# Sums of squares later in TensorE's order, and block 0's keys turned by VectorE and exchanged through DRAM

## The reference

```python
mod = silu(c) @ w_ada + b_ada                    # shift, scale, gate
h = rms_norm(x, norm_g) * (1 + scale) + shift
proj = h @ w_in                                  # u, z_pool, q, k, v, o, z_m, gates: 7 x 512 + 8 columns
pool_out = causal_pool_mixer(u, w_pool, ls_pool) * silu(z_pool)
qk = silu(causal_depthwise_conv(q | k))          # width 4
hm = mlstm_chunkwise(q, k, v, ig, lf)            # 4 heads x 128, chunks of 128 positions
mlstm_out = head_norm(hm) * sigmoid(o) * silu(z_m)
x = x + gate * (concat(pool_out, mlstm_out) @ w_out)
return rms_norm(x, final_g)
```

## Time and profile before

| what | us |
|---|---|
| three runs: median (lowest to highest) | 1813.13 (1810.76 to 1817.83) |
| the profiled execution, whole | 1815.33 |
| its span in the trace | 1813.5 |
| PE busy | 1766.9 (97%) |
| DVE busy | 1070.1 (59%) |
| ACT busy | 600.4 (33%) |
| POOL busy | 272.8 (15%) |
| mean granted clock of TensorE | 0.992 of full |

### The profile page before, as it was taken

One profiled execution on the slowest core, in us unless ns is written; L12 is line 12 of the kernel. 1 busy time (PEld: TensorE's weight loads), 2 busy tenths in 40 slices (PEclk: granted clock), 3 DMA queues, 4 the chain that ended last, 5 costly groups with the idle time before them and its releaser, 6 DMA issues.

```text
span 1813.5 us, 25007 instructions
## 1 busy us (share of the span) xinstructions
PE 1766.9 (97%) x9129; PEld 1515.1 (84%) x9129; DVE 1070.1 (59%) x2213; ACT 600.4 (33%) x1430; POOL 272.8 (15%) x229
## 2 busy tenths in 40 slices
PE   6999999999999999999999999999999999999998
PEld 5877878888898888988888887888889888898886
DVE  6685685536836288353873458553684627835383
ACT  3345352343523234222432224232342323422221
POOL 3443122040310013000130002200021000300000
PEclk9899999999999999999999999999999999999999
DMA  9796875798557774686748766478664777456652
GB/s 329 269 331 176 233 193 175 185 259 304 140 187 211 209 237 111 215 229 189 214 120 251 229 192 164 163 215 233 205 151 177 215 195 241 125 202 206 189 172 82
DMA packets 392158, 368.32 MB, mean 203 GB/s; under 512 B 256780, under 2 KB 298724, under 8 KB 392036
## 3 DMA queue, kind: packets, MB, share of 16 engines
q1 hardware_dynamic: 376836, 344.05, 62.9%
q10 hardware_dynamic: 15200, 22.68, 4.4%
HBM read 304.59 MB, written 62.06 MB: 202 GB/s over the span
## 4 chain that ended last, share of the span: by engine, by line
PE 68%; DVE 17%; DMA 6%; ACT 3%; issue 3%; SPq 2%; ACTq 0%; POOL 0%; DVEq 0%; POOLq 0%
PE ps_acc L590 19%; PE ps_acc L592 19%; PE ps_acc L591 19%; DMA sb_kT<-hm_kept 2%; DMA sb_x_in<-x 2%; PE ps_kv L590 2%; PE ps_kv L591 2%; PE ps_kv L592 2%; DVE sb_shifted L1714 1%; DMA hm_kept<-sb_kT 1%; DVE sb_silu_zp L1678 1%; PE ps_num L590 1%; DVE sb_kT L1672 1%; PE ps_num L592 1%; DVE sb_acc_cv L1714 1%
## 5 line engine op out<-in xcount | busy, mean ns | idle before, releaser
L590 PE MATMUL ps_acc<-sb_hT_hi,sb_w_split 128*128 128x512 f32 x1536 | 606.2, 395 | 1.4 <-POOL sb_w_split L1196 1.4
L592 PE MATMUL ps_acc<-sb_hT_hi,sb_w_split 128*128 128x512 f32 x1536 | 599.2, 390 | 0.0
L591 PE MATMUL ps_acc<-sb_hT_lo,sb_w_split 128*128 128x512 f32 x1536 | 598.6, 390 | 0.0
L592 PEld LDWEIGHTS ps_acc<-sb_hT_hi,sb_w_split 128*128 128x128 f32 x1536 | 288.6, 188 | 61.0
L590 PEld LDWEIGHTS ps_acc<-sb_hT_hi,sb_w_split 128*128 128x128 f32 x1536 | 288.9, 188 | 60.3 <-POOL sb_w_split L1196 1.5
L591 PEld LDWEIGHTS ps_acc<-sb_hT_lo,sb_w_split 128*128 128x128 f32 x1536 | 289.1, 188 | 57.4
L1207 POOL TENSOR_TENSOR sb_h_rs<-sb_h_var,sb_mhalf 128x4 f32<-128x4 f32 x32 | 40.9, 1279 | 1037.4 <-DVE sb_h_var L1661 1037.4
L1196 POOL TENSOR_TENSOR sb_w_split<-sb_w_raw,sb_w_split 128x512 fp32r<-128x512 f32 (+1 forms) x64 | 88.3, 1387 | 193.8 <-ACT sb_w_split L869 193.7
L1561 DVE SCALAR_TENSOR_TENSOR sb_acc_cv<-sb_shifted,sb_par,sb_acc_cv 128x512 f32<-128x512 f32 x96 | 76.9, 801 | 60.7 <-ACT sb_acc_cv L1038 58.2
L1591 DVE TENSOR_TENSOR sb_oz<-sb_tanh,sb_oz 128x512 f32<-128x512 f32 x32 | 22.2, 693 | 145.2 <-ACT sb_tanh L1054 145.2
L590 PE MATMUL ps_acc<-sb_wo_hi,sb_mixm_hi 128*128 128x512 f32 x256 | 102.9, 402 | 0.0
(11 more groups left out here) (233 smaller groups left out, 2968.8 us busy)
## 6 DMA issues: line engine op xcount, KB each, us to landing
sb_w_split<-w_kept SPq DMA_DIRECT2D x328, 512.0 KB, 4.6
sb_w_split<-w_kept SPq DMA_DIRECT2D x56, 520.0 KB, 4.3
w_kept<-sb_w_split SPq DMA_DIRECT2D x40, 512.0 KB, 5.2
sb_x_res<-x SPq DMA_DIRECT2D x34, 512.0 KB, 5.1
sb_w_raw<-w_in SPq DMA_DIRECT2D x64, 256.0 KB, 4.8
out<-sb_qT SPq DMA_DIRECT2D x32, 512.0 KB, 2.9
sb_x_in<-x SPq DMA_DIRECT2D x112, 128.0 KB, 3.9
sb_ada_raw<-w_ada SPq DMA_DIRECT2D x8, 1024.0 KB, 9.6
```

The costliest lines, as they stand in the source:

```text
L590: pe.matmul(dst, st_hi, mv_hi, start=start, stop=False)
L591: pe.matmul(dst, st_hi, mv_lo, start=False, stop=False)
L592: return pe.matmul(dst, st_lo, mv_hi, start=False, stop=stop)
```

## The change

The sums of squares: `x_sums(0)` of the next block moves from after `numerator_and_update(2)` to between tile u 3 and tile zp 3. `x_sums(1)` stays after `numerator_and_update(3)` but writes to the bank `sco`. `x_sums(2)` and `(3)` move from after `out_p(1)` and `out_p(3)` to between `out_m(2)` and `out_p(2)`, and between `out_m(4)` and `out_p(4)`. With them move, on VectorE, `prep_var(0)` (from ahead of the `k_w` product of chunk 3 to behind `windows(3)`) and `prep_var(2)` and `(3)` (behind `out_var` and `m_low`); `prep_turn(0)` now stands ahead of `y_low(3)`. On ScalarE `prep_scale(2)` and `(3)` move one output tile later, on GpSimd `x_rsqrt(2)` and `(3)` behind the output's `rsqrt`.

The keys of block 0: `keys_transposed` is gone; block 0 does what the other blocks do. VectorE turns the keys at t = 8 to 11, SP writes them (16 DMAs) at m = 33 to 39 and reads them back at m = 41, 45, 49, 53. `load_keys(0, 0)`, which writes `k_w`, waits until all of them are kept and until `fold_mm` has come to 8. The wait for `wout_scaled` moves into `numerator_and_update(0)`, ahead of L806.

```diff
-        x_sums_at = [bro[:, 0:NC]] * 3 + [kv[1][:, 384:384 + NC]]
+        x_sums_at = [bro[:, 0:NC], sco[:, 0:NC], bro[:, 0:NC]] + [kv[1][:, 384:384 + NC]]
...
             def keep_keys(b, h):
-                sp.wait_ge(keys_turned, (b - 1) * NH + (h + 1))
+                sp.wait_ge(keys_turned, b * NH + (h + 1))
...
                 if j == 0:
-                    sp.wait_ge(keys_kept_done, 256 * b)
+                    sp.wait_ge(keys_kept_done, 256 * (b + 1))
+                    if b == 0:
+                        sp.wait_ge(fold_mm, 2 * NH)
...
-                    if m in (33, 35, 37, 39) and not first:
+                    if m in (33, 35, 37, 39):
                         keep_keys(b, (m - 33) // 2)
-                    if m in (41, 45, 49, 53) and not first:
+                    if m in (41, 45, 49, 53):
                         load_keys(b, (m - 41) // 4)
...
                     tile("u", j)
-                    if first:
-                        keys_transposed(j)
+                    if j == 3 and not last_block:
+                        x_sums(b + 1, 0)
                     tile("zp", j)
                     numerator_and_update(j)
-                    if j >= 2 and not last_block:
-                        x_sums(b + 1, j - 2)
+                    if j == 3 and not last_block:
+                        x_sums(b + 1, 1)
...
                     if i > 1:
                         out_m(i)
+                    if i in (2, 4) and not last_block:
+                        x_sums(b + 1, i // 2 + 1)
                     out_p(i)
-                    if i in (1, 3) and not last_block:
-                        x_sums(b + 1, i // 2 + 2)
...
                     if i in (0, 2, 4) and not last_block:
                         prep_hi(b + 1, i)
                         prep_hi(b + 1, i + 1)
+                    if i in (2, 4) and not last_block:
+                        prep_scale(b + 1, i // 2 + 1)
...
-                    if i in (1, 3) and not last_block:
-                        prep_scale(b + 1, i // 2 + 2)
...
-                    if i in (1, 3) and not last_block:
-                        x_rsqrt(b + 1, i // 2 + 2)
                     if i % 2:
                         j = i // 2
                         rsqrt(o_var_done, b * NC + (j + 1), o_rs[:, j % 2:j % 2 + 1], o_var[:, j % 2:j % 2 + 1], o_rs_done)
+                    if i in (1, 3) and not last_block:
+                        x_rsqrt(b + 1, i // 2 + 2)
...
-                    if 8 <= t < 12 and not first:
+                    if 8 <= t < 12:
                         in_turn()
                         V.transpose(keys_squared[t - 8].rearrange("p (c n) -> p c n", n=P), kT[:, :, t - 8, :]).then_inc(keys_turned, 1)
...
-                    if first:
-                        dve.wait_ge(k_T, j + 1)
-                        keys = kv[1][:, :].rearrange("p (h d) -> p h d", d=P)
-                    else:
-                        dve.wait_ge(keys_loaded[j % 2], 16 * ((b - 1) * 2 + (j // 2 + 1)))
...
-                y_low(3)
                 if not last_block:
                     prep_turn(b + 1, 0)
+                y_low(3)
```

More of the change, by code:

```diff
@@ L268, in build @@
         tanh_ready, qk_ready, o_tanh = sem("tanh_ready"), sem("qk_ready"), sem("o_tanh")
-        pooled_ready, k_T, d_exp, k_w_ready = sem("pooled_ready"), sem("k_T"), sem("d_exp"), sem("k_w_ready")
+        pooled_ready, d_exp, k_w_ready = sem("pooled_ready"), sem("d_exp"), sem("k_w_ready")
         num_done, kv_done, h_ready, c_done = sem("num_done"), sem("kv_done"), sem("h_ready"), sem("c_done")
@@ L783, in heads_to_scores @@
                     last.then_inc(sco_full, 1)
-                def keys_transposed(j):
-                    if j == 0:
-                        pe.wait_ge(wout_scaled, KT)
-                    reach(pe, c_done, j)
-                    for h in range(NH):
-                        last = pe.transpose(kv[1][:, chunk(h)], kT[:, j, h, :], ident)
-                    last.then_inc(k_T, 1)
                 def numerator_and_update(j):
@@ L804, in numerator_and_update @@
                     pe.wait_ge(k_w_ready, b * NC + (j + 1))
+                    if first and j == 0:
+                        pe.wait_ge(wout_scaled, KT)
                     for h in range(NH):
@@ L1118, in one_block @@
                         act.wait_ge(shifted_free, b * 8 + 8)
-                        reach(act, keys_kept_done, 256 * b)
+                        act.wait_ge(keys_kept_done, 256 * (b + 1))
                     act.activation(shifted[:, 0, HALO:], src[:, :], ACT.Copy).then_inc(free, 1)
@@ L1592, in one_block @@
                         did(free, b * (TASKS // 2) + (TASK[name, i] // 2 + 1))
-                    if 8 <= t < 12 and not first:
+                    if 8 <= t < 12:
                         in_turn()
                         V.transpose(keys_squared[t - 8].rearrange("p (c n) -> p c n", n=P), kT[:, :, t - 8, :]).then_inc(keys_turned, 1)
-                        did(keys_turned, (b - 1) * NH + (t - 7))
+                        did(keys_turned, b * NH + (t - 7))
                     if t == 0:
@@ L1755, in one_block @@
                         head_norm(j - 1)
-                    if j == 3 and not last_block:
-                        prep_var(b + 1, 0)
                     in_turn()
-                    if first:
-                        dve.wait_ge(k_T, j + 1)
-                        keys = kv[1][:, :].rearrange("p (h d) -> p h d", d=P)
-                    else:
-                        dve.wait_ge(keys_loaded[j % 2], 16 * ((b - 1) * 2 + (j // 2 + 1)))
-                        keys = kT[:, j - 1, :, :] if j else k_w[:, :, :]
-                    V.tensor_tensor(k_w[:, :, :], keys, rows(expo[:, 1, NH * j:NH * j + NH]), ALU.mult).then_inc(k_w_ready, 1)
+                    dve.wait_ge(keys_loaded[j % 2], 16 * (b * 2 + (j // 2 + 1)))
+                    V.tensor_tensor(k_w[:, :, :], kT[:, j - 1, :, :] if j else k_w[:, :, :], rows(expo[:, 1, NH * j:NH * j + NH]), ALU.mult).then_inc(k_w_ready, 1)
                     did(k_w_ready, b * NC + (j + 1))
@@ L1771, in one_block @@
                     if j == 0:
-                        reach(dve, keys_kept_done, 256 * b)
+                        dve.wait_ge(keys_kept_done, 256 * (b + 1))
                     windows(j)
+                    if j == 3 and not last_block:
+                        prep_var(b + 1, 0)
                     if j == 2:
@@ L1832, in one_block @@
                         out_norm(i // 2 - 1)
-                    if i in (1, 3) and not last_block:
-                        prep_var(b + 1, i // 2 + 2)
                     if i % 2:
@@ L1841, in one_block @@
                         m_low(2 + i // 2)
+                    if i in (1, 3) and not last_block:
+                        prep_var(b + 1, i // 2 + 2)
                     if i == 2:
```

## The result

The changed kernel takes 1821.76 us (median of 10 runs, 1819.71 to 1824.66), the kernel before 1812.51 us (median of 10, 1809.81 to 1817.83). The ratio is 1.0042, 95% interval 1.003 to 1.0053: slower by some 7.6 us by this ratio, 9.25 us by the two medians. That is inside the wide range of 1805 to 1824, but 5.8 us above the 1816 that was forecast and just outside the forecast's own range, 1811 to 1821. The profiled execution of the changed kernel took 1820.55 us, with a span of 1818.7 us against 1813.5.

A forecast was written before the change was run, and what follows sets the result against it. TensorE, busy 97% of the span, was taken as the bound. From the profiled 1815.33 us, + 5.2 (block 0) - 0.9 (steady waits) - 3.1 (clock) gave 1816.5; forecast 1816, own range 1811 to 1821, wide range 1805 to 1824.

The forecast's parts named there:

- The bound and what takes its place: Blocks 1 to 6, out tile 2: x_sums waits go, add_residual(0) ends next; gain capped at 4.25 us, 0.9 us kept.
- The shift on VectorE: Block ends: prep_turn(0) ahead of y_low(3) makes everything behind it 0.65 us later, or 1.15 with the longer x_rsqrt.
- TensorE's own time: Later places of x_sums have room: x_sums(2) comes 2.7 us behind its old place, the longest wait was 2.55.
- The clock: Block 4: the fall to 1.2 GHz for 6.2 us after a 2.55 us wait goes; 3.1 us gained.
- The pair of gaps that was forecast for block 4: Block 4: one gap becomes two, 1.1 us at out_p(0) and about 1.4 at out tile 2.
- The bound that 2.20 us pass without a fall: After block 0's 2.20 us wait the granted clock stayed 1.00, so block 4's shorter new gaps should not lower it.
- Block 0: SyncE's queue: load_keys(0, 0) holds raw units 42 and 43, delaying out tile 2 to 272.05; 5.2 us lost (4.5 to 9.0).
- Unit 42's own delay: Block 0: its load lands 5.5 us after issue, so its split comes at 198.0, 6.5 us late (5.8 to 10.3).
- The keys' other costs: Block 0: four VectorE transposes and 16 stores by SyncE, taken as 0 us, bounds 0 to 2.8.
- (A): Rival, plain gain: block 0's delay hidden and nothing comes in place of the waits; 1799.2 us, chance 0.13.
- (B): Rival, slower by the clock: new gaps drop TensorE to 1.2 GHz in block 0 and two steady blocks; 1825.8 us, chance 0.13.
- (C): Rival: squares of part 2 still end last at the new place and the waits stay; 1820.5 us, chance 0.06.

The follow-up runs named there:

- the sums alone: Against the kernel before: only the sums of squares and what moves with them on VectorE, ScalarE and GpSimd moved; block 0's keys stay with TensorE; ratio 0.9995.
- the run with part 0 early: Changed kernel with x_sums(0), x_sums(1) and prep_var(0) in their old places, prep_turn(0) still ahead of y_low(3); ratio 1.0001 to the kernel before.
- the load behind x: Changed kernel with block 0's first load of keys issued behind raw units 42, 43 and the next x's eight loads; ratio 0.9998 to the kernel before.

## Why the prediction came out as it did

**The bound and what takes its place.** Right. TensorE's waits at `x_sums` went and waits for `add_residual(0)` came: 5.0 us in six places. Steady blocks were to give 0.9 + 3.1 = 4.0 us; the profiled pair gives 3.6. But that agreement is partly luck. Block by block the differences are +1.18, +0.43, +0.30, -5.38, +0.49 and -0.63, where 0.2 to 0.5 of gain and one block at -3.1 were forecast. The step treated one execution's waits, 0.70, 0.66, 2.55 and so on, as if the next execution had them again; they hang on the wait for the heads, which differs from block to block and between executions. The half with the sums alone, 0.9995 (0.9985 to 1.0004) or 1 us, is the better measure of this step. It fits the 0.9; the 4.0 with the clock's 3.1 lies outside it (0.9985 is 2.7 us).

**The shift on VectorE.** Right to the hundredth. In block 2 the instructions ahead of the old place of `prep_var(0)` stand 10.57 us later than before, those behind the pair of transpose and `y_low(3)` 11.21: 0.64, forecast 0.65, and in the other blocks it is the same within 0.02. `x_rsqrt(0)` took 1.01, as taken, and the Trainium skill's rule ("SBUF — State Buffer", "Who interferes with whom") gives the same: no contention beside an instruction with at most one SBUF input. In the run with part 0 early, back beside the `k_w` product, it took 1.51 again. What was missing is that the 0.65 could have been avoided by leaving part 0 early; the run with part 0 early shows it.

**TensorE's own time.** Missed, small. `x_sums(0)` now stands between two tiles of 24 matmuls, and `add_residual(3)` and `(5)` end just as TensorE arrives. The matmul that they release is 0.50 us long, and the next one starts 0.33 after it instead of 0.23. In block 2, `add_residual(3)` ends at 722.55 and out tile 5 begins at 722.60. The prediction said that the later places of `x_sums` have room; behind them, at out tiles 5 and 7, none is left, though nothing longer than 0.15 us came of it.

**The clock.** Block 4's fall went, for a different reason (its wait for heads was 0.62). The pair of gaps that was forecast for block 4 shows in block 5 instead, where the wait for heads was 2.67, and the clock stayed at 1.00 in the 6 us from either gap:

```profile
1343.44 0.50 PE L592 MATMUL ps_acc<-sb_wo_hi,sb_mixp_hi 128*128 128x512 f32 x1 [0.39 <-DVE sb_mixp_lo L1681]
1350.34 0.50 PE L592 MATMUL ps_acc<-sb_wo_hi,sb_mixm_hi 128*128 128x512 f32 x1 [1.16 <-DVE sb_x_res L1782]
```

The bound that 2.20 us pass without a fall failed: in block 0 the mean granted clock was 0.71 in the 5.84 us after a wait of 2.21 (window from 264.16 on):

```profile
264.16:270.00 5.84, 5.84 (x18) 4.40 (x19) 4.49 (x13) 4.00 (x10) 1.32 (x2) 0.71 0.35 55
```

With it came one of the prediction's own signs of being wrong, a fall of the clock elsewhere. It cost nothing in this place: TensorE then waited another 0.91 us for `add_residual(0)`, and VectorE waited nowhere for TensorE on its way there.

**Block 0.** The mechanism was right: SyncE, held for `fold_mm`, keeps raw loads back, and the delay goes on to the block's end. The term was mis-sized: 5.2 forecast, 8.75 - 0.4 = 8.4 measured (out tile 2 starts at 275.23 where 272.05 was forecast). Unit 42's own delay, taken as 6.5, was 4.6: its load landed 3.3 us after its issue, under the median of 4.8 that the prediction took as the least. What was left out is that each of x's eight loads costs SyncE 0.8 to 0.9 us to issue, and that they move behind the release too; through them unit 46 is 9.05 us late, and that sets the block. The section on the change names x's loads as standing behind the release; the prediction gave them no price. Two smaller steps were off as well. The 0.83 us of VectorE's idle time before the silu of zp 0 absorbed nothing: that wait is for ScalarE's tanh, which is itself behind the splits, and the whole 9.05 passed through (205.82 to 214.87). And the chain runs on through the raw load behind unit 51 (its split 8.95 us late); unit 51's own split, on which the prediction let it run, is 7.83 late (226.45 to 234.28). The keys' other costs, forecast at nothing, are nothing: with the load behind x the ratio is 0.9998.

**The rivals.** (A) did not come, since `add_residual(0)` was as close as read and block 0's delay was not hidden. (B) has a grain: one fall of the clock, in block 0, without a cost of its own. (C) is refuted; `x_sums` waits nowhere. The total follows: 1816.5 with block 0 at 8.4 instead of 5.2 is 1819.7, beside 1820.55 in the profiled execution. Against the median of before, without a fall of the clock to win back, it is 1812.5 + 8.4 - 0.9 = 1820.0, beside 1821.76.

## What to carry to other kernels

When an issue with a wait is put into a queue, price everything behind it: the issue time of the DMAs that had been issued in a pause counts beside the wait (here 7.3 us). Look back from the wait of the bounding engine to the last place where the engine that it waits for stood idle itself: here that was a DMA round trip some 35 us up, and moving that one wait gave 0.9965, where moving all the sums at the end gave 0.9995. And test the halves of a change apart, since one may be neutral, the other harmful, and a third part of it useful by itself.
